# One-pass layer norms with a pre-centred residual, and the triangular inverse's transpose made by TensorE

## The reference

```
mu  = mean(x, -1);  var = mean((x - mu)**2, -1)
y   = (x - mu) * rsqrt(var + 1e-5) * g + b
```

## Time and profile before

| | us |
|---|---|
| median of 3 runs | 2548.92 |
| profiled execution | 2577.67 |
| its span, first to last instruction | 2575.8 |
| PE busy | 2500.9 (97%) |
| DVE busy | 1722.5 (67%) |
| ACT busy | 1202.0 (47%) |
| POOL busy | 396.0 (15%) |

### The profile page before, as it was taken

The page is one execution under the profiler, slowest core; times in us unless marked ns, Lnnn a source line. Parts: engine busy times, 40 slices in busy tenths (PEclk is TensorE's granted clock), DMA queues, the critical chain, the costliest instruction groups (busy, mean ns, idle before and its releaser), DMA issues.

```text
span 2575.8 us, 51609 instructions
## 1 busy us (share of the span) xinstructions
PE 2500.9 (97%) x20966; PEld 2433.1 (94%) x20966; DVE 1722.5 (67%) x2733; ACT 1202.0 (47%) x1862; POOL 396.0 (15%) x516
## 2 busy tenths in 40 slices
PE   7999999999999999999999999999999998899997
PEld 7999999988899999999999999999999998799996
DVE  6677655675766655655656877677677775577765
ACT  5333334444544444444444555444455543455653
POOL 1233300050200000000002211101101114201104
PEclk9999999999999999999999999999999999799998
DMA  6433335554455556556556554454454444344442
GB/s 217 146 117 115 119 132 181 170 176 154 147 187 188 188 168 203 188 169 205 191 167 182 189 176 156 158 170 162 155 182 154 153 150 145 123 156 148 155 164 92
DMA packets 124502, 418.36 MB, mean 162 GB/s; under 512 B 13796, under 2 KB 17644, under 8 KB 124012
## 3 DMA queue, kind: packets, MB, share of 16 engines
q1 hardware_dynamic: 124268, 415.06, 48.9%
HBM read 412.37 MB, written 3.68 MB: 162 GB/s over the span
## 4 chain that ended last, share of the span: by engine, by line
PE 83%; issue 8%; DVE 4%; POOL 3%; ACT 2%; DMA 1%; SPq 0%; ACTq 0%; POOLq 0%; DVEq 0%
PE b L707 25%; PE b L709 24%; PE b L708 24%; PE b L1052 1%; PE b L686 1%; DVE WL L1541 1%; PE b L836 1%; PE b L822 1%; PE b L833 1%; PE b L1063 1%; DVE t1s L1639 1%; POOL sms L2227 1%; PE b L1104 0%; POOL t1s L2260 0%; POOL t1s L2368 0%
## 5 line engine op out<-in xcount | busy, mean ns | idle before, releaser
L707 PE MATMUL b<-XH,WH 128*128 128x256 f32 x4224 | 1214.8, 288 | 24.9 <-DVE WL L1541 16.0
L708 PE MATMUL b<-XL,WH 128*128 128x256 f32 x4224 | 1184.4, 280 | 0.0
L709 PE MATMUL b<-XH,WL 128*128 128x256 f32 x4224 | 1184.3, 280 | 0.0
L1165 ACT ACTIVATE WH<-WR 128x1024 fp32r<-128x1024 f32 (+2 forms) x811 | 817.0, 1012 | 632.4 <-PE b L709 627.1
L1541 DVE TENSOR_TENSOR WL<-WR,WH 128x1024 fp32r<-128x1024 f32 (+2 forms) x811 | 960.1, 1193 | 19.2 <-ACT WH L1165 18.8
L707 PEld LDWEIGHTS b<-XH,WH 128*128 128x128 f32 x4224 | 798.4, 189 | 42.0 <-issue 21.9
L709 PEld LDWEIGHTS b<-XH,WL 128*128 128x128 f32 x4224 | 806.5, 191 | 0.0
L708 PEld LDWEIGHTS b<-XL,WH 128*128 128x128 f32 x4224 | 800.0, 189 | 3.9 <-issue 3.3
L707 PE MATMUL b<-OH,WH 128*128 128x256 f32 x1680 | 479.7, 286 | 3.8 <-DVE WL L1541 1.7
L708 PE MATMUL b<-OL,WH 128*128 128x256 f32 x1680 | 469.4, 279 | 0.0
L709 PE MATMUL b<-OH,WL 128*128 128x256 f32 x1680 | 469.4, 279 | 0.0
(11 more groups left out here) (370 smaller groups left out, 2194.9 us busy)
## 6 DMA issues: line engine op xcount, KB each, us to landing
WR<-a_w_in SPq DMA_DIRECT2D x160, 512.0 KB, 3.5
WR<-w_in SPq DMA_DIRECT2D x112, 512.0 KB, 3.6
WR<-w_gate SPq DMA_DIRECT2D x88, 512.0 KB, 3.8
WR<-w_up SPq DMA_DIRECT2D x88, 512.0 KB, 4.1
WR<-a_w_out SPq DMA_DIRECT2D x64, 512.0 KB, 3.5
WR<-b_w_in SPq DMA_DIRECT2D x64, 512.0 KB, 3.6
WR<-w_down SPq DMA_DIRECT2D x64, 384.0 KB, 3.5
WR<-w_down SPq DMA_DIRECT2D x64, 320.0 KB, 2.9
```

Of the source, the lines that this page charges most:

```text
L707: mm(ps, WH[:, slot, at:at + P], xh, start=(k == 0), stop=False)
L708: mm(ps, WH[:, slot, at:at + P], xl, start=False, stop=False)
L709: m = mm(ps, WL[:, slot, at:at + P], xh, start=False, stop=(k == p["kt"] - 1))
L1165: act.activation(WH[:, s, 0:n], WR[:, r, 0:n], ACT.Copy).then_inc(*act_w.up(i))
```

## The change

Layer norms, both layers:

- The mean of the residual is taken out early. POOL sums the 16 blocks of the residual before or while the first part of the output projection is added (`add_mid`); PE multiplies the sum with ones (step "mid", "s"), DVE scales it, and DVE subtracts it from each block just before that block is evacuated in a later part ("so" part 1, "bo" part 0; `centred`, 16 instructions of 128x256 per layer).
- Squares and their sum are made during the last part: ACT squares each block after its evacuation (`ln_square`), DVE adds them up (`ln_squares`, 14 adds). Block 15 is left to PE, which adds it in its own matmul.
- "stat" takes the place of "mean" and "tok": two float32 matmuls for the mean, 8 matmuls of one column for the sums of x and x*x per token, four small DVE instructions for the variance as mean of squares less squared mean, the power on POOL. The mean is still subtracted from the 8 pairs (6 on DVE, 2 on POOL).
- "apply": one DVE instruction per block multiplies by gain and by the inverse deviation read from PSUM; the bias is added by ACT (with the write of XH in layer 0, even blocks) and, for even blocks of layer 0, by DVE in the write of XL. The scaling by ALPHA leaves the layer norm: 16 ACT steps, one per slot, behind the first two products.
- Before the layer norm of layer 0 the splits of the next four chunks are completed (`pump(used + 4)`, `low_now`), and the products bkv 0 and 1 run by turns, 4 blocks each (`two`).

The inverse: step "b(l)" makes only 4 matmuls (for T, at l = 6 for the transpose). For levels 1 to 5 the transpose comes from 4 PE transposes of T in step "a(l+1)", copied by ACT.

The diff, cut to its core:

```diff
+    def two(self, keys, name, ms, src, evac):
+        ...
+        for k0 in (0, CK):
+            i = [self.use((name, m, k0, k0 + CK, 1)) for m in ms]
+            for k1 in (k0, k0 + 4):
+                for key, n in zip(keys, i):
+                    self.step("half", key, n, k1, k1 + 4, k0, k1 > k0)
+                    if k1 == 12:
+                        self.evac(key, self.products[key])
+                    self.slot()
...
-    for name in ("mean", "tok", "rows"):
-        q.step("ln", 0, name)
-    for m in range(4):
+    q.pump(q.used + 4)
+    q.low_now()
+    q.step("ln", 0, "stat")
+    q.step("ln", 0, "apply")
+    q.two([("bkv", 0), ("bkv", 1)], "kv_w", (0, 1), 4, "bkv")
+    q.begin(("mid", 1), [("x", m) for m in range(16)] + [None] * 12 + ["s"], 1, 1)
+    for m in (2, 3):
         q.product(("bkv", m), "kv_w", m, 4, 16, "bkv")
... PE, gdn "a" and "b"
                 m.then_inc(*pe_gdn.up("a", pr, l))
+                if l > 1:
+                    transposed(here("t"), [Tmt[:, quarter(u)] for u in range(4)]).then_inc(*pe_gdn.up("t", pr, l - 1))
...
-                if l < 6:
-                    for u in range(4):
-                        mm(to[:, u * 64:(u + 1) * 64], TTt[:, quarter(u)], blocks(pm[:, quarter(u)], l, 0),
-                           start=True, stop=True)
                 for u in range(4):
-                    m = mm(to[:, S + u * 64:S + (u + 1) * 64], pm[:, quarter(u)], blocks(TTt[:, quarter(u)], l, 1),
-                           start=True, stop=True)
+                    if l < 6:
+                        m = mm(to[:, u * 64:(u + 1) * 64], TTt[:, quarter(u)], blocks(pm[:, quarter(u)], l, 0), ...)
+                    else:
+                        m = mm(to[:, u * 64:(u + 1) * 64], pm[:, quarter(u)], blocks(TTt[:, quarter(u)], l, 1), ...)
... ACT, gdn "a"
+                if l > 1:
+                    w.wait_ge(*pe_gdn.of("t", pr, l - 1))
+                    act.activation(blocks(T2(TT), l - 1, 1), blocks(from_bank(name, "t")[:, :], l - 1, 1), ACT.Copy)...
... PE, ln "stat"
+                mm(to[:, 0:S], ones, ACC[:, :], start=True, stop=False)
+                w.wait_ge(*dve_ev.of(("bo", 1, 15) if layer else ("so", 3, 15)))
+                mm(to[:, 0:S], ones, last, start=False, stop=True).then_inc(*pe_ln.up("mean", layer))
...
+                for c in range(2):
+                    mm(to[:, 2 + c:3 + c], squares[:, quarter(c)], ones[:, 0:1], start=True, stop=False)
+                    m = mm(to[:, 2 + c:3 + c], square[:, quarter(c)], ones[:, 0:1], start=False, stop=True)
... DVE, before an evacuation of so part 1 or bo part 0
+            dve.tensor_tensor(XT[:, m, :], XT[:, m, :], RB[:, :] if layer else T1(7), ALU.subtract)...
... DVE, ln "stat" and "apply"
+                centred(0)
+                w.wait_ge(*pe_ln.of("cols", layer))
+                ... (mean and mean of squares, squared mean, variance, epsilon)
+                for m in (2, 6, 8, 12, 14):
+                    centred(m)
...
+                rstd = bank("ln", layer, "apply", "r")[:, 0:S]
+                for m in range(16):
+                    dve.scalar_tensor_tensor(XT[:, m, :], XT[:, m, :], pc("ln_g", 16 * layer + m), rstd, ALU.mult,
+                                             ALU.mult)...
+                    if layer == 0 and m > 1 and m % 2 == 0:
+                        x_low(m - 2)
... ACT, ln "apply" and the scaling by ALPHA
+            for m in range(16):
+                if layer or m % 2:
+                    act.activation(XT[:, m, :], XT[:, m, :], ACT.Identity, bias=bias)...
+                if layer == 0:
+                    if m % 2:
+                        act.activation(XH[:, m, :], XT[:, m, :], ACT.Copy)...
+                    else:
+                        act.activation(XH[:, m, :], XT[:, m, :], ACT.Identity, bias=bias)...
... POOL
+                    if m == 4:
+                        w.wait_ge(*dve_ln.of("ms", layer))
+                        power(SM(21), SM(20)[:, 2:4], 2).then_inc(*pool_ln.up("r", layer))
+            elif layer == 0:
+                for m in range(1, 16, 2):
+                    pool.tensor_tensor(XL[:, m, :], XT[:, m, :], XH[:, m, :].bitcast(F32), ALU.subtract)...
```

More of the change, by code:

```diff
@@ L285, in evac @@
             self.lows.append(("xlow", v, key[-1]))
+        layer = LAYER.get(key[:-1])
+        if layer is not None and 0 < key[-1] < 15:
+            self.lows.append(("lnsq", layer, key[-1]))
         if p["evac"] in ("conv", "gate"):
@@ L312, in project, with low_now @@
         self.low_parts()
+    def low_now(self):
+        self.step("low", self.split - 1)
+        self.lowed.add(self.split - 1)
     def norm(self, v):
@@ L437, in make_plan @@
     q.project("bo", "b_w_out", list(range(8, 16)), 8, part=1)
-    for name in ("mean", "tok", "rows"):
-        q.step("ln", 1, name)
+    q.step("ln", 1, "stat")
+    q.step("ln", 1, "apply")
     q.step("finish")
@@ L1077, in ssm, with mid @@
                 rows(to, SM(19), 2).then_inc(*pe_ssm.up("nr", g))
+        def mid(layer, *name):
+            if name[0] == "s":
+                to = free(("mid", layer, "s", "s"))
+                w.wait_ge(*pool_acc.of("mid", layer, 15))
+                mm(to[:, 0:S], ones, ACC[:, :], start=True, stop=True).then_inc(
+                    *pe_ln.up("mid", layer))
         def ln(layer, name):
-            if name == "mean":
+            if name == "stat":
+                last, squares, square = XT[:, 15, :], T1(6), T1(3)
@@ L1081, in ln @@
                 to = free(("ln", layer, name, "m"))
[L1082 to L1089, removed]
@@ L1463, in rot @@
                 act.activation(T2(0)[:, half(which)], T1(6), ACT.Sin).then_inc(*act_rot.up(which))
-        def ln(layer, name):
[L1466 to L1481, removed]
-                            w.wait_ge(*pe_prod.of(x_last(3)))
-                            act.activation(XH[:, k, :], XT[:, k, :], ACT.Copy).then_inc(*act_x.up(4, k))
-                if layer == 0:
-                    for m in range(16):
-                        w.wait_ge(*(pool_x if m % 2 else dve_x).of(4, m))
-                        act.activation(XT[:, m, :], XT[:, m, :], ACT.Copy, scale=ALPHA).then_inc(*act_res.up("x4", m))
@@ new lines, in mid @@
+        def mid(layer, *name):
+            if name[0] == "x":
+                m = name[1]
+                w.wait_ge(*(pool_x if m % 2 else dve_x).of(4, m))
+                if m % 2:
+                    act.activation(XT[:, m, :], XT[:, m, :], ACT.Copy, scale=ALPHA).then_inc(*act_res.up("x4", m))
+                else:
+                    w.wait_ge(*pool_ln.of("b2"))
+                    act.activation(XT[:, m, :], XT[:, m, :], ACT.Identity, scale=ALPHA, bias=SM(22)[:, m:m + 1]).then_inc(
+                        *act_res.up("x4", m))
@@ L1534, in split, with low @@
         def split(i):
-            i -= 1
-            if i < 0:
-                return
+            if i and i - 1 not in plan.lowed:
+                low(i - 1)
+        def low(i):
             n, r, s = chunk_n(i), i % RAW, i % HL
@@ L1668, in conv_b, with centred @@
                 *dve_cv.up("end", key, also=("n", n)))
+        def centred(name, part, m):
+            layer = 0 if name == "so" else 1
+            w.wait_ge(*dve_ln.of("mid", layer))
+            w.wait_ge(*pool_acc.of("mid", layer, 15))
+            dve.tensor_tensor(XT[:, m, :], XT[:, m, :], RB[:, :] if layer else T1(7), ALU.subtract).then_inc(
+                *dve_ln.up("mid", layer, m))
         def evac(key):
@@ L2160, in rope @@
+                if layer == 0:
+                    x_low(14)
         def rope(label, to, *who):
```

203 lines of the change are left out of this document (123 added, 80 removed), and 4 rows, old and new, of the table BANKS.

## The result

The changed kernel took 2533.3 us (median of 7 executions, 2508.76 to 2541.87), the kernel before 2554.05 us beside it (7 executions, 2547.72 to 2579.43): ratio 0.990, 95% interval 0.986 to 0.994. The forecast was 2507.5 and the range ended at 2523. The profiled execution took 2531.28 us against 2577.67: 46.4 less, where the sum said 41.4. So the trace gained what was forecast and more, and the medians, 20.8 us apart, half of what was forecast. The scatter tells why: the executions of neither kernel lie around one value.

A forecast was written before the change was run, and what follows sets the result against it. PE was taken as the bound, busy 97% of the span. Layer norm 0 24.6, layer norm 1 9.7 and inverse 8.2, less 1.1 for mean matmuls, gave 41.4 us: 2548.92 to 2507.5 us, range 2499 to 2523.

The forecast's parts named there:

- the last of the sum: Profiled execution to median: the 28.75 us between them carried over unchanged, so 2548.92 - 41.4 = 2507.5 us.
- The sum: Whole kernel: 24.6 + 9.7 + 8.2 - 1.1 = 41.4 us saved.
- Inverse: Levels 1 to 5, 20 places: four matmuls (0.84 us) go, four transposes (0.43) come; 8.2 us of PE saved.
- the end of 12: Upper bound of the inverse's saving, 12 us, if a transpose is hidden wholly; the lower bound was 0.
- Rival B: Inverse: PE waits for ACT's late transpose copy, 0.5 us at 20 places; costs 2 us, total 2517.5; chance 0.11.
- Rival C: Inverse, 90 to 350 us: added transposes let PE's clock fall; slower, 2573 us at a quarter of the stretch; chance 0.03.
- Layer norm 0: From T, the last evacuation's end before it, to the second product's end: 24.7 us instead of 49.3, saving 24.6.
- Rival A: Behind layer norm 0: block arrivals pace PE and its clock stays at half; costs 8 us, 2515.5; chance 0.12.
- One end of the working: Layer norm 0's upper bound: PE warm after 3 us, saving 27 us.
- Layer norm 1: From the last evacuation's end: DVE's last instruction after 14.25 us instead of 24.3; 9.7 us saved, ends 7 and 11.
- The moved work: Norm work moved into streaming stages: hidden, taken as 0 with 3 us as an end; "mid" mean matmuls cost 1.1.
- rival D: Streaming stages: moved DVE, ACT and POOL work stalls them by what the norms save, 30 to 40 us; about 2546; chance 0.03.

The follow-up runs named there:

- group 4: One split matmul 12 matmuls into each long row: changed kernel 2505.84 us, kernel before 2550.47, with the new inverse only 2538.97; changed kernel with one cut 2507.43.
- the inverse alone: Kernel before with only the inverse's part of the change: 2541.19 us uncut; with a split matmul inside each of its long rows 2538.97 us.
- Group 3: Split matmul at the head of one or all long rows, both kernels: changed 2503.61 to 2538 us; before, with one, five executions at 2550 to 2558, five at 2576 to 2580.
- group 1: Uncut, beside the kernel before at 2581.36 us: changed kernel again 2533.99, inverse alone 2541.19, norms alone 2546.13, changed kernel with bkv products one after the other 2537.48.
- groups 4 and 5: Cuts inside long rows; the second group, on the changed kernel with 31 cuts: bkv products one after the other 2508.25 us, no extra split before layer norm 0 2506.54.

## Why the prediction missed

*The step that failed* is the last of the sum: "nothing in the change touches the start, so I carry the difference over". The profiled execution stood 28.75 us above the median. I took that for something at the start that any execution would share or not share alike. It was a level of the longest stage, drawn in each execution: on its lower level the changed kernel runs at 2506 to 2509, where the forecast was 2507.5, and on its upper one at 2531 to 2542, with 6 of the 7 executions that made the median of 2533.3. Nothing in the range stood for that, though it could be read beforehand: the working takes 24 matmuls in 2.72 us from the earlier trace rows, 113.3 ns each, and a window of the longest stage would have shown 851 in 100 us, 117.8. A busy share of 100% hid it. That 2507.5 meets the lower level so closely is in part luck: the 2548.92 it starts from lies 3.5 us under that level's median, and the sum is 3.2 short.

*The sum.* 41.4 forecast, 44.6 measured at equal spacing: 8.2 against 11.5 for the inverse, 24.6 + 9.7 - 1.1 = 33.2 against 33.1 for the norms. The term that was mis-sized is the inverse.

*Inverse.* 8.2 forecast, 11.5 measured; the end of 12 was in the bounds. A set of four transposes holds PE for 0.36 us (98.81 to 99.17), not 0.43, and a level takes 4.96 us (97.97 to 102.93). In the kernel before, by the trace, the same level went from 99.11 to 104.61, 5.50; 20 times 0.54 is 10.8. The set that went was also worth more than 0.84: step "b" held PE from 101.41 to the next product matmul, 1.71 us, and now from 100.63 to 101.44, 0.81, so 0.90. The kernel before, behind the earlier trace rows:

```profile
103.12 0.36 PE L707 MATMUL b<-XH,WH 128*128 128x256 f32 x1
...
104.61 1.00 PE L822 MATMUL b<-t2x 128*128 128x64 f32 x8
```

Rival B is out: ACT's copy ended at 99.85 and "b" started at 100.63, and PE waited for ACT nowhere from 90 to 345 us. Rival C is out: clock 1.00 in the whole stretch.

*Layer norm 0.* 24.7 us from T to the end of the second product were forecast, and the evacuation that PE's end released starts at T+24.3: 25.1 us less than the 49.3 of before. Within it errors cancel. DVE's first pair took 1.76 us beside a pair of POOL's, not 0.69, but the five behind it 4.16, not 4.7: the apply began at T+9.5 (9.3 forecast), PE at T+11.3 (10.9). POOL's power took 1.10 us, not 0.72, and cost nothing, since DVE was in its pairs until T+9.6. Against the later start, PE was at half clock for 3.3 us (2172.47 to about 2175.8; the windows have 0.50 until 2175, 0.81 to 2177 and 1.00 from there), not 6, and its 96 matmuls took 12.7 us, not 13.8. POOL's low parts took 0.74 to 0.75 us each, not 1.25; the last ended at T+21.0, as forecast, because each waited 0.50 us for ACT, and never held PE up. Rival A is out. Here the rule of "SBUF — State Buffer", "Who interferes with whom", in the Trainium skill, was the better guide than the middle of the rows. The trace agrees with it: POOL was not slowed beside the applies, while DVE's own low parts, which have two SBUF inputs, took 0.54 to 0.68 us where one of POOL's was under way and 0.47 where none was. One end of the working is also off by its own terms: three us at half clock give T+23.3 and so 26.0, not 27; 25.1 lies inside either.

*Layer norm 1.* 14.25 us to DVE's last instruction forecast, 14.1 seen (2512.28 to 2526.39, with ACT's to 2527.04 behind it), and from the evacuation's end to the end of the span 17.2 us against 27.3: 10.0 less, where 9.7 was forecast.

*The moved work.* The trace of layer norms 0 and 1 gives 25.1 + 10.0 = 35.1 us; the norms' whole part is worth 33.1. The rest, 2.0 us, would be what the moved work costs elsewhere, 1.1 of it the two mean matmuls of "mid" as charged; a trace set against a median that is known to 1.5 us cannot say it closer, but the profiles of group 4 show the same size: the changed kernel comes to T 0.8 us later than the inverse alone and takes 0.5 us longer from the second product to the last evacuation. The cover held: rival D is out.

*What stays open.* What an execution draws from, and why the changed kernel drew the upper level 10 times of 13 and the kernel before 28 of 86. Nothing of the change lies in the row. Its first two matmuls start 0.20 to 0.21 us apart in profiles of both levels alike, and it had its spacing within ten matmuls. Group 3 shows that the odds can move (11 of 22 with cuts at the head, 0 of 23 without), not by what. The inverse alone was never there (6), the two uncut kernels with the new norms mostly (10 of 12), but no run tells this from chance in the chip and the hour. Whether anything but a split matmul would do inside a row was not tried, and why a split one does is not shown.

## What to carry to other kernels

When executions scatter on two levels, count matmuls per window in the longest unbroken stage before any sum is made, and compare kernels level by level or with the level taken out; the median of the kernel before, unedited, moved from 2552.0 us in group 3 to 2581.4 in group 1. Where a kernel streams thousands of equal matmuls, try one cut matmul inside the row, behind a dozen or so that ran unbroken, not at its head. A step that hides a split ahead of a norm is to be priced with what stands behind the norm if it is left out.

## What the hardware showed that was not expected

A row of weight loads and 256-column matmuls on PE runs at one of two spacings, 113.3 or 117.8 ns, at the same granted clock of 1.00 (2.4 GHz), and kept it to the end of a row of 6323. The section "Back-to-back issue gap" of "TensorE: Matmul & The Clock Gate" in the Trainium skill says that the spacing of such a stream is set by weight load and matmul together, and gives one sustained value each for 128 and for 512 columns; the runs here show two for 256. A matmul split into two of 128 columns costs 0.10 us and, 12 or more matmuls into a row, led to the short spacing in every execution timed (none of 40 on the upper level, nor of the 26 with 60 or 152 cuts) and in each of the 131 places of groups 4 and 5 where the row ahead had run unbroken; as the second matmul of a row, or just behind a pause, it did not always.
